# 160 columns between weight blocks, and another order at the end of a Strassen group

## What is computed

```
hn = rmsnorm(x, norm_mix_pre)
m  = mixer(hn)             # even: hn @ w_in_even (1024x2048), gating and RG-LRU, @ w_out_even (1024x1024)
                           # odd:  hn @ c_w_in (1024x3072), short gated convolution, @ c_w_out (1024x1024)
x  = x + rmsnorm(m, norm_mix_post)
hn = rmsnorm(x, norm_ffn_pre)
f  = square(relu(hn @ mlp_up)) @ mlp_down      # 1024x4096, 4096x1024
x  = x + rmsnorm(f, norm_ffn_post)
```

## Time and profile before

| | us |
|---|---|
| median of 3 runs | 2183.42 (2182.91 to 2184.45) |
| profiled execution | 2183.0 |
| its span, first to last instruction | 2181.2 |

### The profile page before, as it was taken

The page is one execution under the profiler, slowest core; times in us unless marked ns, Lnnn a source line. Parts: engine busy times, 40 slices in busy tenths (PEclk is TensorE's granted clock), DMA queues, the critical chain, the costliest instruction groups (busy, mean ns, idle before and its releaser), DMA issues.

```text
span 2181.2 us, 33137 instructions
## 1 busy us (share of the span) xinstructions
PE 2158.2 (99%) x13880; PEld 2146.0 (98%) x13880; DVE 1125.6 (52%) x1702; ACT 704.1 (32%) x1201; POOL 240.1 (11%) x271
## 2 busy tenths in 40 slices
PE   9999999999999999999999999999999999999998
PEld 9999999999999999999999999999999999999998
DVE  7766376324655646334943333394226475564336
ACT  5673354202232322333411112354113223132332
POOL 2000000001120211000033232000003121130000
PEclk9999999999999999999999999999999999999999
DMA  4111432111111111141311113131111111111142
GB/s 164 34 41 40 138 94 65 47 42 49 49 39 50 48 49 49 43 134 46 113 49 49 40 49 128 57 101 49 49 49 41 48 49 49 49 43 45 49 138 80
DMA packets 209059, 138.76 MB, mean 64 GB/s; under 512 B 6640, under 2 KB 205424, under 8 KB 208912
## 3 DMA queue, kind: packets, MB, share of 16 engines
q1 hardware_dynamic: 208192, 135.51, 20.4%
q10 hardware_dynamic: 720, 1.13, 0.1%
HBM read 119.22 MB, written 17.40 MB: 63 GB/s over the span
## 4 chain that ended last, share of the span: by engine, by line
PE 86%; issue 10%; DVE 1%; ACT 1%; DMA 0%; POOL 0%; DVEq 0%; ACTq 0%; SPq 0%; POOLq 0%
PE ps L876 24%; PE ps L877 23%; PE ps L878 23%; PE ps L922 5%; PE ps L925 5%; PE ps L924 5%; PE ps L996 1%; PE ps L1024 0%; ACT w_all L1109 0%; DVE h_lo L1557 0%; PE ps L952 0%; PE ps L943 0%; DMA w_all_raw<-in_w_in_even_dram 0%; PE ps L939 0%; DVE w_all L1463 0%
## 5 line engine op out<-in xcount | busy, mean ns | idle before, releaser
L876 PE MATMUL ps<-x_hi,w_all 128*128 128x352 f32 x2304 | 759.5, 330 | 0.0
L878 PE MATMUL ps<-x_hi,w_all 128*128 128x352 f32 x2304 | 751.6, 326 | 0.0
L877 PE MATMUL ps<-x_lo,w_all 128*128 128x352 f32 x2304 | 751.6, 326 | 0.0
L876 PEld LDWEIGHTS ps<-x_hi,w_all 128*128 128x128 f32 x2304 | 432.6, 188 | 2.7
L877 PEld LDWEIGHTS ps<-x_lo,w_all 128*128 128x128 f32 x2304 | 432.6, 188 | 2.2
L878 PEld LDWEIGHTS ps<-x_hi,w_all 128*128 128x128 f32 x2304 | 432.5, 188 | 0.0
L1109 ACT CAST w_all<-w_all_raw 128x1024 fp32r<-128x1024 f32 (+1 forms) x166 | 194.5, 1172 | 470.0 <-DMA w_all_raw<-in_mlp_up_dram 141.4
L876 PE MATMUL ps<-h_hi,w_all 128*128 128x352 f32 x960 | 310.8, 324 | 0.0
L878 PE MATMUL ps<-h_hi,w_all 128*128 128x352 f32 x960 | 307.9, 321 | 0.0
L877 PE MATMUL ps<-h_lo,w_all 128*128 128x352 f32 x960 | 307.9, 321 | 0.0
L922 PE MATMUL ps<-h_hi,w_all 128*128 128x264 f32 x896 | 256.4, 286 | 13.6 <-issue 9.0
(11 more groups left out here) (229 smaller groups left out, 2214.0 us busy)
## 6 DMA issues: line engine op xcount, KB each, us to landing
w_all_raw<-in_mlp_up_dram SPq DMA_DIRECT2D x60, 512.0 KB, 3.9
w_all_raw<-in_mlp_down_dram SPq DMA_DIRECT2D x64, 256.0 KB, 3.1
w_all_raw<-in_mlp_down_dram SPq DMA_DIRECT2D x28, 512.0 KB, 3.6
x_save<-f SPq DMA_DIRECT2D x9, 1408.0 KB, 6.2
x_old<-x_save SPq DMA_DIRECT2D x9, 1408.0 KB, 12.7
w_all_raw<-in_c_w_in_dram SPq DMA_DIRECT2D x22, 512.0 KB, 3.6
w_all_raw<-in_w_in_even_dram SPq DMA_DIRECT2D x12, 512.0 KB, 3.6
x_old<-in_x_cols_dram SPq DMA_DIRECT2D x3, 1408.0 KB, 12.6
```

Of the source, the lines that this page charges most:

```text
L876: nc.tensor.matmul(dst, wh, hi, start=(i == 0), stop=False)
L877: nc.tensor.matmul(dst, wh, lo, start=False, stop=False)
L878: last = nc.tensor.matmul(dst, wl, hi, start=False, stop=(i == KC - 1))
```

## The change

Two things are changed.

**The gap.** For the panels of `w_in_even`, `c_w_in` and `mlp_up` in a rotating slot the blocks stand 160 columns (640 bytes, 5 units) apart in place of 128, high and low ones alike; the low ones begin 8 x 160 columns into the slot. What multiplies x from `w_s` or from h's memory stays, and so does all that multiplies h. Line numbers move by up to 6.

**The order at a group.** On ACT `t_casts(n)` comes last at unit n: behind the casts of weights. On DVE the low half of unit gs-2 comes behind the evacuation of gs-1 in place of ahead of it; `t32_add` is cut in two, and in the second part T2's sum moves behind the low half of the last unit; `t_low` of T3 and T2 (first part) moves from gs-3 and gs-2 to the end of gs-2, behind the subtraction of pair 1.

```diff
@@ -391,8 +391,9 @@
         def w_views(slot, l):
             if slot in ROTATING:
                 s = ROTATING.index(slot)
-                size = FORMS if LOADS[l].pair else D
-                three = [w[:, s, i * size:(i + 1) * size].rearrange("p (k n) -> p k n", n=P)
+                step = P + 32 if LOADS[l].name[0] in ("w_in_even", "c_w_in", "mlp_up") else P
+                size = FORMS if LOADS[l].pair else KC * step
+                three = [w[:, s, i * size:(i + 1) * size].rearrange("p (k n) -> p k n", n=step)[:, :, 0:P]
                          for w, i in ((w_all, 0), (w_all, 1), (w_all_raw, 1))]
             elif slot == "s":
                 three = [w[:, i, :].rearrange("p (k n) -> p k n", k=KC)
@@ -1427,7 +1428,6 @@
                     up_unit(n)
                 if kind == "us":
                     up_halves(n)
-                t_casts(n)
                 if kind in ("k1", "k2", "k0"):
                     odd_unit(n)
                 if kind in ("eo", "oo", "dn3"):
@@ -1436,6 +1436,7 @@
                 for l in range(4, N_LOADS):
                     if high_at[l - 4] == n:
                         high(l)
+                t_casts(n)
 
             def old_copy(i, a):
                 c0, rows = last_rows(i)
@@ -1560,13 +1561,17 @@
                     last = nc.vector.tensor_tensor(t_form(h_lo_raw, 1, u.m), b12_raw(u.m), b11_raw(u.m), ALU.subtract)
                 last.then_inc(h_ready, 1)
 
-            def t32_add(q, c):
+            def t3_add(q, c):
 
                 t3 = t_form(h_lo_raw, 3, c)
                 dve.wait_ge(h_ready, index[GROUP[q] - (5, 2)[c]] + 1)
                 nc.vector.tensor_tensor(t3, t3, b12_raw(c), ALU.subtract).then_inc(t_sum, 1)
+
+            def t2_add(q, c):
+
                 dve.wait_ge(t_sum, 4 * q + 2 * c + 1)
-                nc.vector.tensor_tensor(t_form(h_lo_raw, 2, c), t3, b11_raw(c), ALU.add).then_inc(t_sum, 1)
+                nc.vector.tensor_tensor(t_form(h_lo_raw, 2, c), t_form(h_lo_raw, 3, c), b11_raw(c), ALU.add
+                                        ).then_inc(t_sum, 1)
 
             def t_low(q, i, c):
 
@@ -1577,22 +1582,23 @@
                                         ALU.subtract).then_inc(t23_ready, 1)
 
             def strassen_before(n):
-                if UNITS[n - 1].kind == "us":
+                if UNITS[n - 1].kind == "us" and n + 1 not in GROUP:
                     halves_low(n - 1)
                 for q, gs in enumerate(GROUP):
                     if n == gs - 4:
-                        t32_add(q, 0)
+                        t3_add(q, 0)
+                        t2_add(q, 0)
+                    if n == gs:
+                        t2_add(q, 1)
 
             def strassen_after(n):
                 for q, gs in enumerate(GROUP):
                     s = n - gs
                     if s == -3:
-                        t_low(q, 3, 0)
                         pair_sums(nc.vector, dve, PAIRS[q][1], w_sum_d, 4 * q)
-                    if s == -2:
-                        t_low(q, 2, 0)
                     if s == -1:
-                        t32_add(q, 1)
+                        halves_low(n - 1)
+                        t3_add(q, 1)
                     if s == 1:
                         t_low(q, 2, 1)
                     if s == 2:
@@ -1941,6 +1947,9 @@
                         low_part(l, low_at[l - 4].index(n), len(low_at[l - 4]))
                     else:
                         low(l)
+                if n + 2 in GROUP:
+                    t_low(GROUP.index(n + 2), 3, 0)
+                    t_low(GROUP.index(n + 2), 2, 0)
 
             n = NORM[3, "post", 2]
             dve.wait_ge(f_sq, 96)
```

## The result

| | us |
|---|---|
| median of 4 runs after | 2148.16 (2148.07 to 2148.38) |
| median of 4 runs before | 2183.32 (2182.91 to 2184.45) |
| ratio | 0.9838, 95% interval 0.9821 to 0.9855 |
| span of the profiled execution | 2146.2 |

What follows compares the result with a forecast made beforehand. The prediction took the step of TensorE's matmuls as the bound (99% busy). Gap 39.7, order 9.6 and half clock 1.7, less 0.3 at the start, gave 50.7 us off 2183.4: 2132.5 us, range 2122 to 2151.

Steps and rivals of the forecast that it cites:

- Part 1, the gap: x units of rotating slots: blocks 160 columns apart alternate the distance's parity every 3 matmuls, gaining 39.7 us, bounds 24 to 47.
- the new step: x units of rotating slots: 159.3 ns per matmul, between bounds 158.3 and 161.7, near the h units' steady 159.
- the first stage: 42 x units where both paces alternate: a gain between nothing and 7.5 us, taken as 2.
- Rival A: x units: the slow entry lasts, 216 units run at 161.5 ns, total 2144 us; chance 25%.
- a pace once taken lasts while nothing disturbs it: Matmul steps on TensorE: distance matters to the step, and a pace, such as 166.7 or 158.3 ns, persists undisturbed.
- Part 2, the order: End of the eight groups: new order cuts TensorE's waits, 9.6 us gained, plus 1.7 from the half clock.
- The wait at `s2`: TensorE before `s2` in each of eight groups: wait becomes 0 to 0.9 us, taken as 0.5; 13.6 becomes 4.
- The half clock: Behind the first group's 2.3 us wait: 3.4 us at clock 0.51 cost 1.7 us and goes with the wait.
- rival C: Group ends: the order only moves the wait; all eight become 2.3 us, half followed by half clock; 2154 us, 6%.
- The start: First four panels, the only ones waited for: their DMAs in smaller pieces cost 0.3 us.
- B: x units: the address does not set the step, so they stay as they are; 2172 us, chance 5%.
- D: All 288 x units: each change of distance is charged, steps 169, 167, 167, mean 167.7 ns; 2190 us, chance 3%.

Runs made afterwards that it cites:

- turned: The changed kernel with the blocks of every second x unit, from a stage's 13th unit on, taken last to first; 2149.49 us (0.9849).
- highshift: The changed kernel without the gap; of blocks multiplying x from rotating slots, high ones 128 and low ones 256 bytes later; 2138.00 us (0.9797).
- even: The changed kernel without the gap; all blocks multiplying x from rotating slots 128 bytes later, so every distance is even; 2139.41 us (0.9805).
- entries: As highshift, but behind each of the eight product groups the next stage's panels take other layouts, the first differing from the rest; 2144.17 us (0.9824).
- fast_tries: As highshift, but all-odd panels behind one highshift panel after products, at once behind h units, and singly elsewhere; last 12 units gapped 16 columns; 2138.38 us (0.9797).
- order_only: The changed kernel with blocks 128 columns apart again, so only the order at the groups is new; 2173.20 us (0.9960).
- lowshift: The changed kernel without the gap; of blocks multiplying x from rotating slots only the low ones 128 bytes later; 2146.33 us (0.9835).
- paces: As fast_tries without its tries; stages beginning with entry slots get one gap panel, one highshift panel, then all-odd ones; 2132.34 us (0.9771).
- gap_only: The kernel before with the gap alone, the order at the groups as it was; 2164.49 us (0.9921).

## Why the prediction was right or wrong

**Part 1, the gap: 26.9 us in place of 39.7.** The direction was right, and so was its ground: the distance's parity sets the step, and no unit of a rotating slot is left at 166.7. The term that failed is the new step, 159.3 ("nearest to the last, since most units lie in long undisturbed stages"). It is 161.1 wherever nothing stands between. I took the h units' steady pace for x because both alternate every three matmuls, and did not ask which operand moves. Had I written own and next distance beside each other for both, the difference was to be seen in the addresses, though no row of before had its price. The bounds, 24 to 47, held; the upper price, 161.7 from the earlier trace rows, was the near one. For the 216 units: 5184 x (166.7 - 161.1) = 29.0; the 30 fast ones lost 720 x 2.8 = 2.0; in the first stage, where the prediction took 2 for a gain, gains and losses nearly cancelled (171.6 us before, 171.5 after).

**Rival A** had nearly the right time (2144) and the wrong reason. It called 161.5 a slow entry that lasts. But units that came from 159 went to 161.1 as well, and turned shows that a break does not end it. Two paces do exist, in the all-odd layout and in highshift, and in `even` in a few units; for the all-odd layout entries and fast_tries showed them chosen by what is ahead. That the time came near rival A's is luck, and it is A's allowance that kept it in the range. That sentence of the prediction, "a pace once taken lasts while nothing disturbs it", is shown for the kernel before.

**Part 2, the order: 9.0 us in place of 9.6 + 1.7.** The wait at `s2`: 0 to 0.9 forecast, 0.5 taken, 0.30 by the profile and 0.46 by the starts (the step at `s2` is 584 ns against 122). The half clock went, as forecast; by the starts it had cost 1.5 us (15 matmuls at 220 or 202 ns in place of 122), not 1.7. What was missed is behind it. Of the kernel after, DVE in the second group:

```profile
634.20 2.45 DVE L1581 TENSOR_TENSOR h_lo<-h_lo_raw,h_hi 128x528 fp32r<-128x528 f32 x2
636.58 0.51 DVE L1624 SCALAR_TENSOR_TENSOR tmp<-ps,rstd 128x352 f32<-128x352 f32 x1
...
638.25 0.52 DVE L1558 TENSOR_TENSOR h_lo<-h_lo_raw,h_hi 128x352 fp32r<-128x352 f32 x1
638.68 0.70 DVE L1573 TENSOR_TENSOR h_lo_raw<-h_lo_raw 128x528 f32<-128x528 f32 x1
639.30 1.32 DVE L1632 TENSOR_TENSOR f<-ps,f 128x528 f32<-128x528 f32 x2
```

and POOL and PE beside it:

```profile
632.73 2.74 POOL L797 TENSOR_TENSOR h_lo<-h_lo_raw,h_hi 128x528 fp32r<-128x528 f32 x1 [3.87 <-ACT h_hi L1191]
```

```profile
635.50 0.28 PE L923 MATMUL ps<-h_hi,w_all 128*128 128x264 f32 x1
```

TensorE left the last `us` unit at 635.50, but its evacuation starts at 636.58, behind the two T subtractions, which took 2.45 us beside POOL's in place of 1.4: the block that I had allowed for. And T2's sum (638.68, 0.6 us) now stands between the low half that lets `s2` go and the products' evacuation (639.30). That evacuation frees the bank of `s3` later by so much, and `s3` waits until 640.76; this is read from the trace, no run moved the sum alone. I had looked behind `s2` as far as `s6`, which is in time, and not at `s3`. This is the wait moved on that rival C spoke of, but of 0.35 us by the starts, not of 2.3. There are now 16 short waits for 8 long ones, and each costs about 0.15 us more than its idle time shows (584 - 122 against 300 ns, 472 - 122 against 190). With that the waits cost 13.6 + 8 x 0.15 = 14.8 before and 3.9 + 16 x 0.16 = 6.5 after: 8.3 saved and not 13.6 - 3.9. With 1.5 of clock this is 9.8; the 0.8 that the products gave back lies in the step behind the new wait (0.07 each) and a product step of 121.9 in place of 121.8.

**The start: 0.7 in place of 0.3.** The four first panels, whose load is waited for, are `w_in_even`; these land in 4.0 us (page, part 6) against 3.6 in the earlier trace rows. The five kernels with a gap for these panels start at 23.6 to 23.9 (landing in 4.0 or 4.1), those without at 22.7 to 23.1 (3.5 or 3.6), but for `lowshift`, at 23.6 without a gap: single executions scatter by as much, so the 0.7 is not all shown to be the gap's.

```profile
w_all_raw<-in_w_in_even_dram SPq DMA_DIRECT2D x12, 512.0 KB, 4.0
```

**Rivals B and D.** B (the address does not matter) is out by even against order_only. D (each change of distance is charged) is right in that the three matmuls with an odd distance climb, but by 161, 162, 164 and not 169, 167, 167, and the even three are at 160 and pay nothing.

**The sum.** 26.9 + 9.0 - 0.1 - 0.7 against 50.7: of the missing 15.6 us 10.7 is the step of the 246 units, 2.1 the first stage, 2.3 the order, 0.5 the start and the entry panels.

What stays open is what in the chip makes a distance odd or even: the runs tell which layouts give which steps, not why, and a shift by half a unit was looked at only in a layout that mixes it with whole ones. What it is that the units of high carry on, so that O behind them goes to one pace or the other, is open too. Nor was a layout tried for the entry panels (161.5 on the mean before, 161.7 after, where nothing stands between) or the products.

## What to carry to other kernels

When TensorE is busy all the time, compute the step from stretches of the trace stage by stage: one mean hid paces of 158 and 167 here. Write down where weights and moving data lie in units of 128 bytes, for each matmul and the one behind it, and try a shift by one unit before anything larger: it costs a few bytes and gave 33.8 us. When one part makes an engine faster, price the other waits again with the new pace, since gap and order apart gave 25.9 us and together 33.7, all against the same 2181.8.

## What the runs showed of the hardware that I had not expected

- A pace has a memory. Units of the same layout run at 158.3 or at 166.7 ns, for as long as 54 units (paces) and 62 (before), and what is ahead decides, further back than three units. It repeated in all eight stages of fast_tries and within 0.5 us over the four runs of paces.
- Even alone is not safe either: in `even` the units n = 42 to 47 and the two at 74, 330 and 426 are at 161.1 by their starts, as are 436 to 438 in fast_tries, against 160.0 elsewhere.
- In the profiled execution of gap_only all eight waits are 2.0 us, and the granted clock fell to half, 1.2 GHz in place of 2.4, behind two of them (rows of 0.50 and, over its edge, 0.70), and not behind the other six.
- The fastest pace of 352 columns, 158.3 ns, and the step of the products of 264 columns, 121.8, differ by 36.5 ns, and 88 columns at 2.4 GHz are 36.7 (an estimate from these two steps and the granted clock): what a matmul takes on top of its columns is about the same, 11.7 ns, for both.
